# Two fused transformer blocks on one core: VectorE's order in the first mixer, and one GpSimd subtraction, are changed

## The reference

```python
h = rmsnorm(x, norm_mix_g)
(lru_x, lru_gate, m_qk, m_v, m_o, m_i, m_f, s_q, s_k, s_v, g_a, g_b, g_c) = split(h @ w_in)
xa = causal_dwconv(lru_x, conv_lru_w)                    # 4 taps
ya = (rg_lru(xa, ...) * gelu(lru_gate)) @ w_out_lru      # a_t h_{t-1} + u_t
qk = silu(causal_dwconv(m_qk, conv_mlstm_w))             # 4 taps, 512 channels
yb = (sigmoid(m_o) * mlstm(qk, m_v, m_i, m_f)) @ w_out_mlstm
yc = stick_breaking_attention(s_q, s_k, s_v) @ w_out_sb  # strict causal mask
x = x + (sigmoid(g_a)*ya + sigmoid(g_b)*yb + sigmoid(g_c)*yc) @ w_o
```

## Time and profile before

| | |
|---|---|
| median of three runs | 764.88 us (764.15 to 765.18) |
| the profiled execution, its own time | 765.51 us |
| its span, first to last instruction | 763.8 us |
| TensorE busy | 753.1 us, 99% of the span, 4305 products |
| VectorE busy | 517.6 us, 68% |
| ScalarE busy | 402.5 us, 53% |
| GpSimd busy | 68.5 us, 9% |
| mean granted TensorE clock | 0.996 |

### The profile page before, as it was taken

The page is one execution under the profiler, slowest core; times in us unless marked ns, Lnnn a source line. Parts: engine busy times, 40 slices in busy tenths (PEclk is TensorE's granted clock), DMA queues, the critical chain, the costliest instruction groups (busy, mean ns, idle before and its releaser), DMA issues.

```text
span 763.8 us, 10432 instructions
## 1 busy us (share of the span) xinstructions
PE 753.1 (99%) x4305; PEld 654.8 (86%) x4305; DVE 517.6 (68%) x588; ACT 402.5 (53%) x508; POOL 68.5 (9%) x78
## 2 busy tenths in 40 slices
PE   9999999999999999999999999999999999999997
PEld 8988788888988888888899888789887988888885
DVE  5857966695656666666769989774547655656554
ACT  6466479643644454444653486663547533444442
POOL 2000002030000000000133422020003000000000
PEclk9999999999999999999999999999999999999999
DMA  9765364546566545665465445365235565555431
GB/s 305 231 197 208 109 231 127 204 140 191 171 228 204 171 166 166 191 208 210 165 218 186 162 144 188 111 239 180 89 112 184 173 221 197 188 178 194 157 133 56
DMA packets 74439, 136.19 MB, mean 178 GB/s; under 512 B 4478, under 2 KB 28952, under 8 KB 74392
## 3 DMA queue, kind: packets, MB, share of 16 engines
q1 hardware_dynamic: 72456, 131.33, 51.6%
q10 hardware_dynamic: 1936, 4.19, 1.7%
HBM read 134.46 MB, written 1.05 MB: 177 GB/s over the span
## 4 chain that ended last, share of the span: by engine, by line
PE 79%; DVE 12%; issue 3%; ACT 3%; SPq 1%; DMA 1%; POOL 1%; DVEq 0%; ACTq 0%; POOLq 0%
PE wide L2025 54%; PE bank L2025 22%; DVE arena L1437 4%; DVE low L1321 3%; PE bank L2143 2%; ACT arena L719 2%; ACT high L719 1%; DMA raw<-in_w_in_dram 1%; POOL low L574 1%; SPq L519 1%; SPq L541 1%; DVE arena L1420 0%; DVE arena L1513 0%; DVE arena L1435 0%; DVE arena L1571 0%
## 5 line engine op out<-in xcount | busy, mean ns | idle before, releaser
L1321 DVE TENSOR_TENSOR low<-raw,high 128x2048 fp32r<-128x2048 f32 (+1 forms) x115 | 259.9, 2278 | 113.4 <-ACT high L719 110.6
L719 ACT ACTIVATE high<-raw 128x2048 fp32r<-128x2048 f32 (+1 forms) x130 | 234.2, 1820 | 124.5 <-PE wide L2025 88.5
L2025 PE MATMUL wide<-act_hl,high 128*128 128x256 f32 (+1 forms) x1184 | 297.3, 330 | 0.0
L2025 PE MATMUL wide<-act_hl,low 128*128 128x256 f32 x832 | 235.6, 283 | 0.1
L2025 PEld LDWEIGHTS wide<-act_hl,high 128*128 128x128 f32 x1184 | 199.9, 190 | 22.4
L2025 PE MATMUL wide<-high,act_hl 128*128 128x512 f32 (+1 forms) x560 | 177.9, 391 | 2.0 <-DVE low L1321 1.2
L2025 PEld LDWEIGHTS wide<-act_hl,low 128*128 128x128 f32 x832 | 158.2, 190 | 1.2 <-issue 0.2
L2025 PEld LDWEIGHTS wide<-high,act_hl 128*128 128x128 f32 x560 | 104.9, 189 | 25.8 <-issue 3.2
L2025 PE MATMUL wide<-low,act_hl 128*128 128x512 f32 (+1 forms) x280 | 108.0, 386 | 0.0
L2025 PE MATMUL bank<-high,hid_l 128*128 128x512 f32 x216 | 84.7, 392 | 0.2 <-DVE hid_l L1636 0.2
L2025 PE MATMUL bank<-high,hid_h 128*128 128x512 f32 x216 | 84.3, 390 | 0.0
(11 more groups left out here) (208 smaller groups left out, 674.1 us busy)
## 6 DMA issues: line engine op xcount, KB each, us to landing
raw<-in_w_ff_dram SPq DMA_DIRECT2D x32, 1024.0 KB, 5.3
raw<-in_w_in_dram SPq DMA_DIRECT2D x28, 1024.0 KB, 5.2
raw<-in_w_ffn_in_dram SPq DMA_DIRECT2D x44, 512.0 KB, 4.9
raw<-in_w_ffn_out_dram SPq DMA_DIRECT2D x11, 1024.0 KB, 6.5
raw<-in_w_xkv_dram SPq DMA_DIRECT2D x8, 1024.0 KB, 5.0
raw<-in_w_o_dram SPq DMA_DIRECT2D x4, 1024.0 KB, 5.0
raw<-in_w_out_dram SPq DMA_DIRECT2D x4, 1024.0 KB, 6.3
raw<-in_w_xq_dram SPq DMA_DIRECT2D x4, 1024.0 KB, 5.0
```

The costliest lines, as they stand in the source:

```text
L719: return act.activation(dst, src, func, **k)
L1321: tt(part(low, g), part(raw, g), f32(part(high, g)), SUB).then_inc(sem.low_by_dve, 1)
L2025: return pe.matmul(dst, lhs, rhs, start=start, stop=stop, skip_group_check=loose)
```

## The change

No computation is added or removed. In the first mixer these steps take other places in VectorE's list: `vectors` moves into `if_rows`, ahead of its wait for the logarithm, and with it goes the extra `split_low` (group 6) that stood ahead of `scaled_in`; the first tap of `mlstm_conv` moves to just behind `if_rows`, the other three to behind `ahead_of_half("vo", 1)`; `lru_input` moves ahead of `mlstm_scores`; the strict mask becomes a step of its own, behind `ahead_of_half(("gate", 3), 0)`. TensorE's `sb_sums` starts one row block later inside group 18. In the second block GpSimd makes the subtraction of group 75 before `ln_rstd` and not after it.

```diff
 # GpSimd's list
             ahead_of("za", "T")
+            ahead_of("v2", "T")
             ln_rstd()
-            ahead_of("v2", "T")
 # VectorE, if_rows
                 ts(rows[0:4, 1, :], bank[6][0:4, 0:T], if_bias[:, 0:1], None, ADD).then_inc(sem.if_rows, 1)
+                vectors()
                 dve.wait_ge(sem.log_f, me.seen("log_f"))
 # VectorE, sb_scores
                     stt(sb_a[:, h, :], bank[4 + h][:, 0:DIAG], 0.0, sb_a[:, h, :], MAX, ADD).then_inc(sem.sb_sp, 1)
+
+            def sb_masks():
                 dve.wait_ge(sem.consts, 4)
                 dve.wait_ge(sem.sb_sp, me.seen("sb_sp", 4))
 # VectorE's list
             ahead_of_half("qk", 1)
-            vectors()
-            split_low(me.used + LEAD + 1)
             scaled_in((m_x[:, 0:2, 3:], m_x[:, 2:4, 3:]), sem.qk_in, 1.0)
             ahead_of("ifsv", "T")
             ahead_of_half("vo", 0)
             if_rows()
+            mlstm_conv(range(0, 1))
             ahead_of_half("vo", 1)
+            mlstm_conv(range(1, 4))
             ahead_of_half("sqk", 0)
             mlstm_cols()
             ahead_of_half("sqk", 1)
             scaled_in((s_q, s_k), sem.sqk_in, 0.125, 1.0)
-            mlstm_conv(range(0, 2))
             ahead_of_half(("gate", 0), 0)
-            mlstm_conv(range(2, 4))
             mlstm_qk()
             ahead_of_half(("gate", 0), 1)
+            lru_input()
             mlstm_scores()
-            lru_input()
             ahead_of(("gate", 1), "T")
...
             sb_scores()
             ahead_of_half(("gate", 3), 0)
+            sb_masks()
             sb_halves()
 # TensorE's list
-            products(("gate", 4), "T", at={2: sb_sums})
+            products(("gate", 4), "T", at={3: sb_sums})
```

## The result

The changed kernel takes 765.85 us in the median of 22 runs (764.39 to 768.91), the kernel before 764.28 in 22 runs beside it (763.66 to 765.41): ratio 1.0024, 95% interval 1.0018 to 1.0031, so 1.6 us slower. The profiled execution of the changed kernel took 765.82 us with a span of 764.1 us, 0.3 us more than that of before. Instructions behind the edits have moved by one to three lines.

The account below looks back on a forecast made before the run. TensorE, busy 99% of the span, bounds the kernel, so only its waits can pay. Terms -4.4 + 0.2 + 2.9 + 1.3 = 0.0 us against the profiled 765.51; median set at 764.6, range 760.4 to 766.8.

Parts of the forecast that it names:

- The four mixer waits: First mixer, TensorE waiting for VectorE: 0.49 us at `qk`, 0.77 at `mlstm_qk`, 1.08 at group 14, 0.42 at group 18; all go.
- Group 20: First mixer: ScalarE gets there less early than TensorE, slack of 1.9 us about used up; a loss of 0 to 0.3 us.
- the old stretch: First mixer, behind the wait at group 14: TensorE at half clock, costing 1.66 us, taken to go; 0 to 1.66 kept.
- The new stretch: Second block, behind TensorE's wait ahead of `moba_values(0)`: half clock, taken as +1.3 us out of 0 to 1.66.
- That VectorE is not held: Second block: GpSimd's moved subtraction does not hold VectorE's convolution; -4.4 - 0.7, about 760 us; chance 0.17.
- That the new stretch stays away: Second block: no half clock comes behind the wait ahead of `moba_values(0)`; -1.3 us more, 763.3 us; chance 0.20.
- Late groups 9, 10 and 20: First mixer: vectors delay ScalarE's run and TensorE waits for group 10, or group 20 is short; 1 to 1.5 us; chance 0.12.
- the other side: First mixer: late subtractions take 1 to 1.5 us of its gain; with the second block's +4.2, 766.2 us or more; chance 0.12.
- the case without a hold: Second block: GpSimd's subtraction misses VectorE's convolution, TensorE's 0.70 us wait is won; 760.4 us, the range's low end; chance 0.17.
- The 1.08 us at group 14: First mixer: TensorE's wait for VectorE goes because `lru_input` runs ahead of the scores; 1.08 us.
- two row blocks: First mixer, group 18: 2.7 us of products would not quite cover masks, rounding and `sb_halves`, some 2.8 us; three (4.1) would.
- The hold itself: Second block: GpSimd's subtraction holds one VectorE convolution instruction, VectorE 4.3 us late, `moba_values(0)` 2.9 us later.

Follow-up runs that it names:

- experiment 12: Kernel before, with four 128x128 products that nothing reads put into TensorE's wait at group 14: 764.13 us, ratio 0.9994.
- Experiment 1: Changed kernel with GpSimd's subtraction of group 75 put back behind `ln_rstd`, the first mixer's new order kept: 761.16 us, ratio 0.9955.
- Experiment 5: Changed kernel with ten 128x128 products that nothing reads put into TensorE's wait ahead of `moba_values(0)`: 764.65 us, ratio 0.9998.
- experiment 2: Kernel before, with only GpSimd's subtraction of group 75 moved ahead of `ln_rstd`: 769.56 us, ratio 1.0063.
- experiments 7: Changed kernel with GpSimd's old order put back and `lru_input` again behind `mlstm_scores`: 761.27 us, ratio 0.9955.
- experiment 8: Kernel before, with only `lru_input` moved ahead of `mlstm_scores`: 764.39 us, ratio 1.0002.
- experiment 11: Changed kernel with GpSimd's old order put back and `sb_sums` again ahead of row block 2, not 3: 761.14 us, ratio 0.9957.
- experiment 4: Changed kernel with VectorE's `za_in`, `moba_scores(1)` and `ln_apply` put ahead of the convolution tiles `conv_dw(20, 24)`: 766.79 us, ratio 1.0023.
- experiment 6: Changed kernel with GpSimd's old order, VectorE's `za_in`, `moba_scores(1)` and `ln_apply` ahead of later convolution tiles, group 77 subtracted by VectorE: 760.38 us, ratio 0.9944.

## Why the prediction was wrong

**The working up to the sum was right.** The four mixer waits went. `mlstm_qk` was done at 71.68 (foreseen near 71.9), `lru_input` ran from 73.80 to 80.26 (74.2 to 80.6), the scores were done at 82.25 (82.5), groups 14 and 15 by 86.65 (87). Group 20 cost 0.07 us (0 to 0.3 foreseen). In the second block, with 4.4 us taken off the predicted times: GpSimd from 441.21 to 445.97 (441.2 to 445.9), VectorE late by 8.00 - 3.62 = 4.4 us (4.3), the turns at 450.30 (450.2), the reductions done at 452.04 (452.0), `moba_turned(0)` at 459.95 (459.9), a wait ahead of `moba_values(0)` of 2.55 + 0.16 = 2.7 us (2.4), then half clock. The sum for the profiled executions was 0.0, and +0.3 was measured; term by term -4.2 against -4.37, +2.9 against +3.13 and +1.3 against +1.62.

**The step that failed** is the one from the profiled execution to the median: "Since either slow stretch may be absent from an execution, and its absence gains more after than before, I set the median at 764.6." It starts from a sum that takes the old stretch off in full, and treats the old and the new one as if both were there about as often. Two things were mis-sized in it.

- The old stretch, 1.66 us of the mixer's 4.4, is in 13 of 57 executions of before; the profiled one (765.51) was among them, and it stood 0.6 us above the median of the three runs then known, which was a sign that not all of them had the stretch. The median of before has none of it (experiment 12), so against the median the mixer is worth its waits, 2.71 us by the traces, and not 4.37. Experiment 1 measured 3.3, with an interval of 2.5 to 4.4.
- The new stretch was entered with 1.3 out of 0 to 1.66, with a chance of 0.20 that it doesn't come at all. By the mean clock, half clock was in 18 of 22 executions, and nine of them stand higher than one stretch explains. The upper end of that term should have been 3 us: the group at 767.5 stands 2.8 us above the one without any.

With the terms as the median has them, -2.71 + 3.13 + 1.62 = +2.0 us, 766.3; with experiment 1's 3.3 in place of 2.71 it is +1.4; measured +1.6. The runs without any half clock stand where -2.71 + 3.13 puts them, +0.4: 764.70, the middle of the four, against 764.28. Experiment 5, which fills the wait, stands at +0.2.

**Rivals.** That VectorE is not held fell with experiment 2. That the new stretch stays away gave its time of 763.3 from the old stretch's 1.66 as well, so it was too low. Late groups 9, 10 and 20 didn't occur. The time I gave to the other side, 766.2 or more, was reached by nine runs, but not through those groups; what those runs lose is open (below). The time of the case without a hold mixes two scales: 765.51 - 5.1 = 760.4 is for the profiled execution, the median would be 759.8.

**Two side claims of the mixer** didn't hold either. The 1.08 us at group 14 were put down to the recurrence's input; experiments 7 and 8 take them from it and leave them to the convolution. And two row blocks would have covered the masks and halves (experiment 11), since the sums need only the first half to start. Neither changed the sum. The stretch of the recurrence's input is 89.28 - 82.78 = 6.50 us, and not 6.46; nothing rests on it.

**The hold itself** was foreseen with its size, by the earlier trace rows. Experiments 1 and 2 show that the hold, with the half clock behind it, is the whole loss; experiment 4 that taking the convolution out from under one subtraction can put it under the next; experiment 6 that with no convolution under a subtraction there, and the early statistics, both waits go.

**Open.** What decides whether a wait is followed by half clock: in the profiled executions waits of 1.39 us (experiment 8), 1.26 us (the turns after) and 1.10 us (experiment 2) were not, one of 1.08 was, so length alone doesn't decide it. Where the runs at 767.5 us lose another 1.8 us: no profiled execution of the changed kernel fell among them. Experiment 5 shows that it goes when this wait is filled. Experiment 4's trace has one stretch of about twice the length (clock 0.70 from 461 to 462 us, 0.50 to 468, 0.88 to 469); that the runs at 767.5 us have one like it, or two short ones, was not seen. The runs with one stretch stand 0.9 to 1.3 us above those without, less than the 1.62 to 1.66 in the traces, and what gives the rest back wasn't looked for.

## What to carry to other kernels

A loss that comes and goes between executions (here a stretch of half clock) is no constant of the sum: read from the times of all runs how often it is there, compare the profiled execution's own time with the median, and give old and new occurrence each its own odds. Before a subtraction is moved on GpSimd, list VectorE's instructions in the time where it will land. Here an instruction with two SBUF operands (4.73 us for 0.48) and a `TENSOR_SCALAR` (2.28 for 0.41) were held to its end, while readers of PSUM (1.91 us for four) and reductions (1.81 us) were not. Whoever moves the VectorE work instead must look at GpSimd's next instruction too. Undo each part of a change alone: here five of six moves were worth 3.3 us, one cost 5.1, and two of the five were worth nothing when undone.

## What was not expected of the hardware

Run times of one kernel fell into groups, at 764.7, 765.6 and 767.5 us, the lowest with the full clock and the others with less, and twenty matmuls of 0.12 us that nothing reads left a single group, 763.91 to 765.27, although the wait stayed as long. A 128x128 product of fp32 operands issued as two matmuls, 0.23 to 0.24 us together (4.63 us for 20, 2.40 for 10). And a wait of about 1.1 us at the same place, in kernels with the same order of work there, was followed by 3.6 us at half clock in one profiled execution (1.08 us, clock 0.54) and by none in another (1.10 us, clock 1.00).
